# First mixing layer: the convolution's running sum is kept in the SBUF tile that is stored at the end, not in PSUM

## The reference

```python
def even_mixer(h, hist_pool, hist_conv, start_pos, w_in, pool_w, pool_scale, conv_w, conv_b, ln_g, ln_b, w_out):
    z = jnp.einsum('btd,de->bte', h, w_in)
    a_in, a_gate, b_val, b_glu, b_gate = jnp.split(z, ...)         # five parts of 1024 columns
    a = multiscale_pool_minus_self(concat([hist_pool, a_in]), start_pos)   # windows 2/4/8/16
    a = jnp.einsum('btgc,gce->btge', a, pool_w).reshape(Bn, T, W_A) * pool_scale
    a = a * silu(a_gate)
    v = b_val * sigmoid(b_glu)
    c = causal_dwconv(concat([hist_conv, v]), conv_w) + conv_b     # each channel: 31 taps over time
    c = silu(layernorm(c, ln_g, ln_b)) * silu(b_gate)
    y = jnp.einsum('bte,ed->btd', concat([a, c]), w_out)
    return y, a_full[:, -15:], v_full[:, -30:]
```

## Time and profile before

| | |
|---|---|
| median of 3 runs | 2813.68 us |
| the profiled execution, its span | 2816.85 us, 2815.1 us |
| TensorE busy (matmul) | 2574.7 us, 91% |
| VectorE busy | 1270.9 us, 45% |
| GpSimd busy | 898.6 us, 32% |
| first mixing layer, first half (convolution) | from 82 to 693 us of the span |
| line 882 (taps 1 to 30), 240 instructions | 308.9 us of VectorE |

### The profile page before, as it was taken

One profiled execution on the slowest core, in us unless ns is written; L12 is line 12 of the kernel. 1 busy time (PEld: TensorE's weight loads), 2 busy tenths in 40 slices (PEclk: granted clock), 3 DMA queues, 4 the chain that ended last, 5 costly groups with the idle time before them and its releaser, 6 DMA issues. The chain is left out here.

```text
span 2815.1 us, 36797 instructions
## 1 busy us (share of the span) xinstructions
PE 2574.7 (91%) x14846; PEld 2431.6 (86%) x14846; DVE 1270.9 (45%) x1366; ACT 414.6 (15%) x688; POOL 898.6 (32%) x842
## 2 busy tenths in 40 slices
PE   4999998997676899998899999999999996999996
PEld 4999998996676697796899999999999996689776
DVE  5898969788654423223422223132322225322324
ACT  3111101112113201102200000000000013210112
POOL 2433332331225332333333333333323336133232
PEclk7999999998887899999999999999999997999998
DMA  2211211112121322330111111111111103132231
GB/s 91 72 61 46 66 56 55 62 54 95 69 80 49 101 79 64 112 100 31 45 43 46 42 45 45 41 45 44 42 45 42 44 23 109 46 116 70 76 108 64
DMA packets 224275, 177.54 MB, mean 63 GB/s; under 512 B 10786, under 2 KB 217322, under 8 KB 224154
## 3 DMA queue, kind: packets, MB, share of 16 engines
q1 hardware_dynamic: 215194, 162.21, 18.8%
q10 hardware_dynamic: 8984, 14.00, 1.4%
HBM read 157.71 MB, written 19.40 MB: 63 GB/s over the span
## 5 line engine op out<-in xcount | busy, mean ns | idle before, releaser
L144 POOL TENSOR_SCALAR w_hi<-w_raw 128x512 fp32r<-128x512 f32 x404 | 284.7, 705 | 1763.3 <-PE PS L205 1516.0
L205 PE MATMUL PS<-h_hi,w_hi 128*128 128x364 f32 x2880 | 643.8, 332 | 29.1 <-ACT e_GS L701 12.7
L205 PE MATMUL PS<-h_hi,w_lo 128*128 128x364 f32 x2880 | 641.3, 331 | 0.0
L205 PE MATMUL PS<-h_lo,w_hi 128*128 128x364 f32 x2880 | 639.7, 331 | 0.0
L147 POOL TENSOR_TENSOR w_lo<-w_raw,w_hi 128x512 fp32r<-128x512 f32 x404 | 543.9, 1346 | 33.7
L205 PEld LDWEIGHTS PS<-h_hi,w_hi 128*128 128x128 f32 x2880 | 500.9, 190 | 32.2 <-issue 14.6
L205 PEld LDWEIGHTS PS<-h_hi,w_lo 128*128 128x128 f32 x2880 | 505.3, 190 | 0.0
L205 PEld LDWEIGHTS PS<-h_lo,w_hi 128*128 128x128 f32 x2880 | 503.3, 189 | 0.0
L205 PE MATMUL PS<-y_hi,w_hi 128*128 128x364 f32 x1200 | 274.4, 338 | 80.5 <-DVE y_lo L946 40.4
L882 DVE SCALAR_TENSOR_TENSOR PS<-e_V,prm,PS 128x1024 f32<-128x1024 f32 x232 | 298.7, 1288 | 6.6
L205 PEld LDWEIGHTS PS<-y_hi,w_hi 128*128 128x128 f32 x1200 | 212.4, 194 | 87.2 <-DVE y_lo L946 41.6
(11 more groups left out here) (181 smaller groups left out, 2176.2 us busy)
## 6 DMA issues: line engine op xcount, KB each, us to landing
w_raw<-in_w_in_odd SPq DMA_DIRECT2D x128, 256.0 KB, 2.8
w_raw<-in_w_in_even SPq DMA_DIRECT2D x80, 256.0 KB, 2.9
a_KV<-in_cache_mem_k SPq DMA_DIRECT2D x64, 256.0 KB, 4.9
a_KV<-in_cache_mem_v SPq DMA_DIRECT2D x64, 256.0 KB, 3.6
w_raw<-in_w_out_even SPq DMA_DIRECT2D x32, 256.0 KB, 2.9
w_raw<-in_w_k SPq DMA_DIRECT2D x32, 256.0 KB, 2.7
w_raw<-in_w_v SPq DMA_DIRECT2D x32, 256.0 KB, 3.0
w_raw<-in_w_q SPq DMA_DIRECT2D x32, 256.0 KB, 2.8
```

What stands on the lines that cost most here:

```text
L144: c.nc.gpsimd.tensor_scalar(c.Wh[:, s, :], c.Wraw[:, s % RAW, :], 1.0, 1.0, ALU.mult, ALU.mult).then_inc(self.w_hi, 1)
L205: mm = pe.matmul(ps[:, q, 0:PART], w, a[:, q * PART:(q + 1) * PART], start=first and n == 0, stop=last and n == 2)
```

## The change

The running sum goes straight into `CB[:, j % 2, 0:T]`, the SBUF tile that tap 30 wrote before. `SUMS` is gone. Tap 0 reads V and writes the tile; taps 1 to 30 read V and the tile and write the tile. As tap 0 now writes the tile of block j - 2, it waits from block 2 on for that block's store. No instruction is added, removed or moved on any engine; only operands differ, and that one wait.

```diff
         AT = SG[:, 0:184].rearrange("p (b t) -> p b t", b=NB)
-        SUMS = c.PS[:, 6:8, :].rearrange("p a n -> p (a n)")
         G = Gemm(c, sem)
...
                     if n == 0:
                         wait_read(dve, ("val", j))
-                        v.tensor_scalar(SUMS, V[:, 0:T], tap, c.prm[:, j, ROW_CONV_B:ROW_CONV_B + 1],
+                        if j >= 2:
+                            dve.wait_ge(stored[j % 2], 16 * (j // 2))
+                        v.tensor_scalar(CB[:, j % 2, 0:T], V[:, 0:T], tap, c.prm[:, j, ROW_CONV_B:ROW_CONV_B + 1],
                                         ALU.mult, ALU.add).then_inc(cv, 1)
                     else:
                         dve.wait_ge(cv, TAPS * j + n + (0 if n <= SAMPLE_AT else 5))
-                        v.scalar_tensor_tensor(CB[:, j % 2, 0:T] if n == CONV - 1 else SUMS, V[:, n:n + T], tap, SUMS,
+                        v.scalar_tensor_tensor(CB[:, j % 2, 0:T], V[:, n:n + T], tap, CB[:, j % 2, 0:T],
                                                ALU.mult, ALU.add).then_inc(cv, 1)
```

## The result

| | before | after |
|---|---|---|
| median, lowest to highest (us) | 2814.43, 2811.77 to 2817.13 (4 runs) | 2845.76, 2844.25 to 2847.67 (4 runs) |
| ratio | 1 | 1.0112, 95% interval 1.0094 to 1.0129 |
| span of the profiled execution | 2815.1 us | 2845.9 us |
| from the first `value` (at 82.2 us) to `sum` | 610.7 us | 639.1 us |

The change costs 31 us, 1.1%; forecast were 40 us. Of the 30.8 us by which the span grew, 28.4 lie before the tile `sum`.

What follows compares the result with a forecast made beforehand. VectorE and TensorE, both near their limits, alternately pace the convolution stage. Terms -4.7 - 1 + 39.4 + 3 + 1 + 2 = +39.7 us gave a forecast of 2853 us, 1.4% slower, range 2832 to 2874 us.

Steps and rivals of the forecast that it cites:

- Where VectorE paces and where it waits: Convolution stage: VectorE paces from the even block's samples' convolution to the odd block's `pooled_low`; then TensorE paces.
- the five stretches: Where VectorE paces: one in each of groups 0 to 2, two in group 3; 31.5 GpSimd units hit taps there.
- the new one before `agate`: A new TensorE wait forecast before the odd block's `agate`, where `value` is now late; no size given.
- Tap 0, -4.7 us: 8 instructions writing SBUF instead of PSUM: 0.58 us less each, all on the path, -4.7 us.
- Taps by themselves, 6 ns less: Taps 1 to 30, 240 instructions: 6 ns less each, 1.4 us in all, 1 us taken on the path.
- Beside GpSimd, 39.4 us: Taps with two SBUF inputs take turns with GpSimd: 31.5 units split in the five stretches, 1.25 us each, +39.4 us.
- The growing chain, 3 us: While VectorE's chain of taps grows, TensorE works on and calls for more GpSimd units: +3 us.
- Outside the five stretches: Rest of the stage: taps among `outa` additions and behind `pooled_low` mostly hidden in VectorE's waits.
- the end of group 0, +1: 17 taps at group 0's end, about 4 us of hits against some 3 us of cover: +1 us.
- Cover in groups 1 and 2: VectorE's 14 and 11 us of waiting there hide the hits on other taps; 12 us more if cover were gone.
- Clock, +2 us: Longer and new waits bring more stretches of lower TensorE clock: 0 to 19 us, 2 us taken.
- The new wait, GpSimd's delay: Tap 0's wait for the store of block j - 2, and GpSimd finishing units up to 2 us later: 0 us each.

Runs made afterwards that it cites:

- experiment 5: Kernel before, with the running sum in SBUF only for 62 taps' input, where VectorE should have time; tap 0 in PSUM: 2816.34 us against 2813.38, ratio 1.0009.
- experiment 6: Kernel before, with the running sum in SBUF for the other taps (167 with two SBUF inputs), tap 0 in PSUM: 2850.22 us, ratio 1.0132.
- Experiment 4: Kernel before, with only tap 0 writing the SBUF tile, tap 1 reading it and writing PSUM: 2814.32 us against 2816.79, ratio 0.9991.
- experiment 2: Changed kernel, with GpSimd splitting only 8 of 512 columns of units 4 to 95: 2784.93 us, ratio to the kernel before 0.9884.
- experiment 1: Kernel before, sum in PSUM, with GpSimd splitting only 8 of 512 columns of units 4 to 95: 2789.78 us, ratio 0.9899.
- experiment 7: Kernel before, sum in PSUM, with ScalarE making tap 0 and half of `add_stats` moved ahead of tap 1: 2798.52 us, ratio 0.9952.

## Why the prediction was right, by its steps

- *Where VectorE paces and where it waits*: shown by experiments 5 and 6. In the five stretches VectorE's work grew by 32.2 us and the stretches by 32.6. TensorE's waits grew where forecast and the new one before `agate` appeared; their sum reached 67.9 us and not 80. The groups grew by 8.8, 10.2, 4.2 and 5.3 us; forecast were 12 for group 0 and 6 to 11 for each other, so three of the four lie below.
- *Tap 0, -4.7 us*: it takes 803 ns, not 753, so 8 x 0.53 = 4.3 us. The row of the second mixer has one pointer operand, this one two (tap and bias). That the second one costs the 50 ns was not tried. Experiment 4 agrees with the sign and the size, but by itself can't be told from no change.
- *Taps by themselves, 6 ns less*: the median is 1285 ns against 1290. The Trainium skill's fixed part (58 cycles from SBUF against 120 from PSUM, "VectorE: DVE Perf Modes", the TRN2 errata) gives 65 ns, an estimate; this trace does not agree, as rows 3 and 4 had said before.
- *Beside GpSimd, 39.4 us*: the taps in the five stretches grew by 38 us. In the chain of block 2 a unit costs 1.16 us where I said 1.25. This is the term that carried the forecast, and experiment 2 shows its cause.
- *The growing chain, 3 us*: there were no more units. Counted in the traces, line 147 begins 55 times in the five stretches, after as before, since TensorE does the same tiles in them.
- *The neighbours* were not in the sum. I counted new meetings as added to the old ones. But a unit held up by a tap may reach `y_low` too late to hold it up. The kernel before paid 27 us for such meetings (experiment 1), and part of this came back: in the five stretches 38.2 us of taps less 2.7 for five tap 0 would be 35.5, and VectorE grew by 32.2, so 3.3 us.
- *Outside the five stretches* I had about +1 us (three tap 0, -1.7; the end of group 0, +1; the clock, +2), and this part got 4.2 us shorter. *Cover in groups 1 and 2* held: the taps in this part grew by 15 us and it did not get longer in sum, and in the profile of experiment 5 the stage did not either.
- *Clock, +2 us*: in the stretches where VectorE paces the granted clock is lower (0.95 instead of 1.00 in group 1), which costs nothing visible there; in two pieces where TensorE paces it is higher, 1.00 instead of 0.96, and they are 2.5 us shorter together. There the sign was wrong; for the whole stage the clock's share was not separated.
- *The mis-sized terms* are therefore these. The sum had 39.7 us, all of it in the stage, and the stage grew by 28.4. Of the 11 us between them 3 are the growing chain, 3.3 the neighbours, and some 5 the rest of the stage. Another 2.4 us of the span's growth arise behind the stage, between about 2380 and 2445 us, where nothing was changed; what they are stays open. That the forecast missed the total by 9 us and not by 11 is owed to them, and so to luck.
- *The new wait, GpSimd's delay*: no wait of VectorE for a store appears, and TensorE waits nowhere for `w_lo` in the stage.

## What to carry to other kernels

The taps with one input in PSUM run beside GpSimd undisturbed (1290 ns at most); moving that input to SBUF makes the instruction itself no dearer (1285 ns) and still makes it wait for GpSimd, here 1.16 us for each unit. Before moving an accumulator, look in the trace for the same form beside a busy GpSimd, and multiply by GpSimd's units in the stretches where VectorE paces, not by the number of VectorE's instructions. And look at what the neighbours already pay: such meetings move as well as add. What did shorten the time, with the sum left in PSUM, was less work for VectorE in these stretches (experiment 7, 14.9 us).

## What was not expected of the hardware

- Turn-taking with GpSimd is not in proportion to its work: the mean tap grew by 59 ns with 256 columns and by 154 ns more with the other 256. GpSimd's line 147 with 8 columns waits (692 ns instead of 287), and beside such units no tap takes over 1303 ns.
- The kernel before, with its sum in PSUM, lost 27 us (1.0%) to such meetings. A copy of 128x64, with one SBUF input, took 661 ns on average and takes 196 without them.
- ScalarE writes 128x1024 from SBUF to PSUM in 1.21 us, with a scale and a bias per partition, faster than VectorE's 1.34 us for the same.
